# A two-layer encoder on one core: the overflow loop moved into the experts' block, and the last turn's activations moved ahead of a weight split

## The chip, the cores and the metric

The kernel runs on one core of a Trainium2 chip. The metric is the device time of one execution in microseconds. Before the change three runs gave 2638.07, 2639.89 and 2648.47 us, median 2639.89 us.

## What is computed

Layer 0 is differential attention beside a Hyena operator, layer 1 a bidirectional mLSTM. Each layer ends with the same mixture of experts, and only that part is touched:

```python
def hier_moe(x, wg, bg, we, be, w1, w3, w2):      # 1024 tokens of 1024, 4 groups x 8 experts, 2 per token
    ...
    def expert_block(args):
        xe, e = args                              # one block: 128 tokens of one expert
        hid = jax.nn.silu(xe @ w1[e]) * (xe @ w3[e])
        return hid @ w2[e]
    yb = lax.map(expert_block, (xb, blk_e)).reshape(cap, d)
    out = jax.ops.segment_sum(yb * buf_gate[:, None], buf_tok, num_segments=t)
    return out
x = x + hier_moe(rms_norm(x, ffn_norm[layer]), ...)
```

Every expert gets one block of 128 slots. An expert with more than 128 tokens needs another block; such further blocks are the overflow.

## The kernel before

The program is a row of phases. A phase is a block with one hand-written instruction stream for each engine, ordered by semaphores. A phase ends with the block's own join of all engines and then `end_phase()` (lines 108 to 111), a barrier of all engines in which the phase's semaphores are cleared. The phase `experts` (line 1886) is followed by the phase `overflow` (line 2226), once in each layer. After layer 0's overflow comes `ml_values` (line 2391), which begins by reading back the sum that the experts have added to in DRAM; after layer 1's the program ends.

**The experts' phase** takes 32 turns, one for each expert. Per turn GpSimd gathers 128 token rows of `xn_scratch` (`fetch`), TensorE transposes them (`turn_x`), and the weights come in three chunks of 2 MB through a ring of three slots, loaded by SyncE (L1948). Precision is kept by splitting: ScalarE makes the high part of each half chunk (`split`, L2119), VectorE the rest (L2172), and TensorE takes three products, L2038 (high by high), L2040 (rest of x by high) and L2046 (high by rest of w). `silu`, `multiply` and `turn_hid` (L2064) make the transposed hidden activations in PSUM; ScalarE's `move_hid` (L2141) writes `hidH`, VectorE's `move_hid` (L2172, `hidL`) the rest. The output product of expert e runs one turn late. ScalarE scales the result into `y` (`store_y`, L2130), and GpSimd adds it to the rows in DRAM with a scatter (`give`: an index copy at L1999 after the scatter before has landed, then the scatter at L2003).

**The last turn's tail.** After expert 31's gate products only its output product is left. ScalarE's `tail()` (L2159) does in order: split of the last chunk's first half, `store_y` of expert 30, split of the second half, `move_hid` of expert 31, `store_y` of expert 31. VectorE's `tail()` (L2210) does: first half, `multiply`, second half, `move_hid`. TensorE can start its 24 output matmuls only when `hidL` is there; the second 12 also need the second half.

**The queues.** SyncE, behind its ring loads, loads the first overflow expert's three weight chunks (L1975) and, in layer 0, three chunks for the next phases (L171), each after VectorE has finished with the ring slot that it overwrites. GpSimd gathers the first overflow block's rows at L2021, before the last four scatters. So the first overflow block's data are asked for during the experts' phase. The overflow phase waits in GpSimd for all scatters to have landed (`given`, L2277). Then each engine reads the count n of overflow blocks from `ctrl` into a register (L2244), branches (L2245), and loops n times: 8 transposes (L2309), two copies, 16 matmuls in full fp32 that show as 32 in the trace (L2318), silu and product (L2344, L2357), 4 transposes (L2323), a copy, 8 matmuls that show as 16 (L2331), two scalings (L2346, L2361) and one scatter (L2293). While it runs, SyncE loads the next expert's weights and GpSimd gathers the next rows, needed or not. The trace shows that n is 0 in layer 0 and 1 in layer 1: L2309 and its followers run once, near 2600 us.

Of the kernel before, what the change touches and what calls it, by code (L numbers as in the profile page):

```python
# [10 lines left out]
ALU = mybir.AluOpType  # L11
# [3 lines left out]
P = 128  # L15
D = 1024
# [60 lines left out]
def build(nc, I, out):  # L77
    ctx = ExitStack()
    with ctx:
# [1806 lines left out]
        def experts(layer, slots, slot_gate, ctrl, total, xg, y, yidx, oidx, w_over):  # L1886

            (idx_ok, x_lo, x_hi, xh_ok, xl_ok, w_high, w_rest, w_used, silu_ok, hid_ok, h_turned, hh_ok, hl_ok,
             y_moved, met, yidx_ok) = take(16)
            got, gave = gather_in, 16 * NE * layer  # L1890
            got_base = list(gathered)
            s0 = S_MOE1 if layer else S_MOE0
            with ExitStack() as st:
# [10 lines left out]
                LAST = NE - 1  # L1904

# [38 lines left out]
                with nc.Block() as block:  # L1944
# [35 lines left out]

                    @block.gpsimd
                    def _(pool_e):
# [43 lines left out]
                        for e in range(NE - 4, NE):  # L2026
                            give(e % 2, e)

# [78 lines left out]

                    def quarter(bank):
                        return psum[:, bank, :].rearrange("p (k t) -> p k t", k=4)

                    @block.scalar
                    def _(act):
# [53 lines left out]
                        run(act, one, tail)  # L2166

                    @block.vector
                    def _(dve):
# [46 lines left out]
                        run(dve, one, tail)  # L2216
                for b in range(2):
                    gathered[b] += 16 * (NE // 2)
# [3 lines left out]
                end_phase()  # L2222

        @phase
        def overflow(layer, slots, slot_gate, ctrl, total, xgs, idx, w):
            (idx_ok, x_turned, xt_lo, xt_hi, h_ok, silu_ok, hid_ok, h_turned, h_moved, y_ok, ye_lo, ye_hi,
             met) = take(13)
            put = over_given[layer]
            w_in = over_w[layer]  # L2230
            got = over_in[layer]
            with ExitStack() as st:
                nm = str(layer)
                xg = xgs[:, 0, :]
                xgT = sb(st, "oxgT" + nm, [P, KD, P])
                act_h = sb(st, "oact_h" + nm, [P, DE])
                hid = sb(st, "ohid" + nm, [P, DE])
                hidT = sb(st, "ohidT" + nm, [P, 4, P])
                y = sb(st, "oy" + nm, [P, D])

                def run(eng, one, last=None):
                    n = eng.value_load(ctrl[0:1, 0:1], min_val=0, max_val=OVER)  # L2244
                    with eng.If(n > 0):  # L2245
                        with eng.Fori(0, n) as i:
                            one(i)
                            eng.wait_ge(put, 16 * (i + 1))  # L2248
                            eng.sem_inc(met, 1)
                    if last:  # L2250
                        last(n)

                def quarter(bank):
                    return psum[:, bank, :].rearrange("p (k t) -> p k t", k=4)

                with nc.Block() as block:
                    @block.sync
                    def _(sp):
                        def one(i):
                            e = sp.value_load(ctrl[0:1, bass.ds(i + 2, 1)], min_val=0, max_val=NE - 1)  # L2260
                            sp.wait_ge(h_ok, i + 1)
                            for c in range(2):
                                sp.dma_start(w[c], expert_src(layer, e, c)).then_inc(w_in[c], 16)
                            sp.wait_ge(y_ok, i + 1)
                            sp.dma_start(w[2], expert_src(layer, e, 2)).then_inc(w_in[2], 16)

                        def last(n):
                            for c in range(3):
                                sp.wait_ge(w_in[c], 16 * (n + 1))
                                sp.sem_inc(met, 1)  # L2270

                        run(sp, one, last)

                    @block.gpsimd
                    def _(pool_e):

                        pool_e.wait_ge(given, 16 * NE * (layer + 1))  # L2277

                        def one(i):
                            nc.gpsimd.tensor_copy(idx[:, 0:1], slots[:, bass.ds(i + NE, 1)]).then_inc(idx_ok, 1)  # L2280
                            nc.gpsimd.tensor_copy(idx[:, 1:2], slots[:, bass.ds(i + NE + 1, 1)]).then_inc(idx_ok, 1)
                            pool_e.wait_ge(idx_ok, 2 * (i + 1))
                            pool_e.wait_ge(x_turned, i + 1)
                            pool_e.sem_inc(met, 1)
                            pool_e.indirect_dma_start(
                                out=xg, out_offset=None, in_=xn_d[:, :],
                                in_offset=bass.IndirectOffsetOnAxis(ap=idx[:, 1:2], axis=0),
                                bounds_check=T - 1, oob_is_err=False
                            ).then_inc(got, 16)
                            pool_e.wait_ge(ye_lo, i + 1)  # L2290
                            pool_e.wait_ge(ye_hi, i + 1)
                            pool_e.sem_inc(met, 1)  # L2292
                            pool_e.indirect_dma_start(  # L2293
                                out=total[:, :], out_offset=bass.IndirectOffsetOnAxis(ap=idx[:, 0:1], axis=0),
                                in_=y[:], in_offset=None, bounds_check=T - 1, oob_is_err=False,
                                compute_op=ALU.add).then_inc(put, 16)

                        def last(n):
                            pool_e.wait_ge(got, 16 * (n + 1))
                            pool_e.sem_inc(met, 1)  # L2300

                        run(pool_e, one, last)

                    @block.tensor
                    def _(pe):
                        def one(i):
                            pe.wait_ge(got, 16 * (i + 1))
                            for k in range(KD):
                                ins = nc.tensor.transpose(psum[:, k // 4, (k % 4) * P:(k % 4 + 1) * P],  # L2309
                                                          xg[:, k * P:(k + 1) * P], ident[:])  # L2310
                            ins.then_inc(x_turned, 1)
                            pe.wait_ge(xt_lo, i + 1)
                            pe.wait_ge(xt_hi, i + 1)
                            for c in range(2):
                                wc = w[c].rearrange("p (k c) -> p k c", k=8)
                                pe.wait_ge(w_in[c], 16 * (i + 1))
                                for k in range(KD):
                                    ins = nc.tensor.matmul(psum[:, 2 + c, :], xgT[:, k, :], wc[:, k, :],  # L2318
                                                           start=(k == 0), stop=(k == KD - 1))
                            ins.then_inc(h_ok, 1)  # L2320
                            pe.wait_ge(hid_ok, i + 1)
                            for k in range(4):
                                ins = nc.tensor.transpose(psum[:, 4, k * P:(k + 1) * P], hid[:, k * P:(k + 1) * P],  # L2323
                                                          ident[:])
                            ins.then_inc(h_turned, 1)
                            pe.wait_ge(h_moved, i + 1)
                            wc = w[2].rearrange("p (k c) -> p k c", k=4)
                            pe.wait_ge(w_in[2], 16 * (i + 1))
                            for half in range(2):
                                for k in range(4):  # L2330
                                    ins = nc.tensor.matmul(psum[:, 5 + half, :], hidT[:, k, :],  # L2331
                                                           wc[:, k, half * 512:(half + 1) * 512],
                                                           start=(k == 0), stop=(k == 3))
                            ins.then_inc(y_ok, 1)

                        run(pe, one)

                    @block.scalar
                    def _(act):
                        def one(i):  # L2340
# [950 lines left out]
```

## Time and profile before

| what | value |
|---|---|
| median of three runs | 2639.89 us (2638.07 to 2648.47) |
| the profiled execution | 2641.77 us |
| its span in the trace | 2639.9 us |
| TensorE busy | 2399.5 us, 91% |
| VectorE busy | 1823.8 us, 69% |
| ScalarE busy | 1449.9 us, 55% |
| GpSimd busy | 482.4 us, 18% |
| mean DMA rate | 205 GB/s |
| mean granted TensorE clock | 0.95 of full |

Shares of busy time are means over phases with different limits. The chain that ended last starts at 2598.92 us, at the start of layer 1's overflow. Rows are read in microseconds from the start of the span; a granted clock of 1.00 is 2.4 GHz and 0.50 is 1.2 GHz.
### The profile page before, as it was taken

The numbers are of one execution on the slowest core, as the hardware profiler recorded it, in microseconds if no ns is written. First come the engines' busy times: TensorE is split into PE (matmuls) and PEld (weight loads), VectorE is DVE, ScalarE is ACT, GpSimd is POOL, SyncE is SP. The second block draws the span as 40 slices with busy tenths as digits, with TensorE's granted clock in tenths as the row PEclk, the third lists the DMA queues.
The fourth block names the chain that finished last, engine by engine and source line by source line (L and its number), as shares of the span: only waits on it lengthen the run. The fifth ranks groups of instructions, "written<-read, shape, count | busy, mean of one in ns | idle before, by whom it ended". The sixth has DMA issues, their size and how long they took to land. (4 is left out here: it accounts for less than half of the span.)

```text
span 2639.9 us, 32620 instructions
## 1 busy us (share of the span) xinstructions
PE 2399.5 (91%) x11612; PEld 1970.5 (75%) x11612; DVE 1823.8 (69%) x2101; ACT 1449.9 (55%) x1777; POOL 482.4 (18%) x431
## 2 busy tenths in 40 slices
PE   7989989796979999999987998997987999999995
PEld 6768877585867888888865786785776888888882
DVE  6838856578348989888963141478547889888880
ACT  6338742322217878777853231266415788877770
POOL 0001100100002333333310000035201333333220
PEclk9989999897979999999998999998997999999997
DMA  5110011111237999999992221101335999999994
GB/s 177 58 40 1 1 48 36 72 32 37 112 128 304 389 374 394 375 380 387 387 383 93 72 72 56 47 19 46 143 134 213 376 379 382 375 379 388 386 387 155
DMA packets 85912, 542.32 MB, mean 205 GB/s; under 512 B 18996, under 2 KB 22677, under 8 KB 59830
## 3 DMA queue, kind: packets, MB, share of 16 engines
q1 hardware_dynamic: 64358, 502.93, 48.5%
q0 software_dynamic: 19008, 33.61, 5.2%
q10 hardware_dynamic: 2448, 4.46, 0.5%
q8 instruction: 62, 1.02, 0.2%
q14 instruction: 36, 0.29, 0.0%
HBM read 521.52 MB, written 55.05 MB: 218 GB/s over the span
## 5 line engine op out<-in xcount | busy, mean ns | idle before, releaser
L2172 DVE TENSOR_TENSOR wL<-ring,wH 128x2048 fp32r<-128x2048 f32 x384 | 869.4, 2287 | 144.0 <-ACT wH L2119 139.4
L2119 ACT CAST wH<-ring 128x2048 fp32r<-128x2048 f32 x384 | 730.5, 1911 | 213.7 <-DMA ring<-in_moe_w 157.5
L2038 PE MATMUL psum<-wH,xgH 128*128 128x512 f32 x1024 | 407.9, 398 | 12.8 <-DVE xgL L2172 12.6
L2040 PE MATMUL psum<-wH,xgL 128*128 128x512 f32 x1024 | 401.3, 392 | 0.0
L2046 PE MATMUL psum<-wL,xgH 128*128 128x512 f32 x1024 | 275.9, 391 | 0.0
L2038 PEld LDWEIGHTS psum<-wH,xgH 128*128 128x128 f32 x1024 | 193.5, 189 | 56.4 <-DVE xgL L2172 12.5
L2046 PEld LDWEIGHTS psum<-wL,xgH 128*128 128x128 f32 x1024 | 193.4, 189 | 40.8
L2040 PEld LDWEIGHTS psum<-wH,xgL 128*128 128x128 f32 x1024 | 193.8, 189 | 38.2
L2038 PE MATMUL psum<-wH,hidH 128*128 128x512 f32 x512 | 208.1, 406 | 11.0 <-DVE hidL L2172 11.0
L2040 PE MATMUL psum<-wH,hidL 128*128 128x512 f32 x512 | 201.7, 394 | 0.0
L1985 POOL COPY gidx<-slots 128x1 int32 (+1 forms) x60 | 56.1, 935 | 485.8 <-PE psum L2055 485.8
L2046 PE MATMUL psum<-wL,hidH 128*128 128x512 f32 x512 | 138.5, 393 | 0.0
L200 PE MATMUL psum<-xn_high,ring_rest 128*128 128x512 f32 x320 | 127.3, 398 | 0.0
L2038 PEld LDWEIGHTS psum<-wH,hidH 128*128 128x128 f32 x512 | 97.7, 191 | 30.6 <-DVE hidL L2172 11.4
L198 PE MATMUL psum<-w_high_route_rest,y_high_route 128*128 128x512 f32 x256 | 105.8, 413 | 12.3 <-DVE ring_rest L193 11.7
L2046 PEld LDWEIGHTS psum<-wL,hidH 128*128 128x128 f32 x512 | 97.3, 190 | 20.4
L2040 PEld LDWEIGHTS psum<-wH,hidL 128*128 128x128 f32 x512 | 97.8, 191 | 18.6
L200 PE MATMUL psum<-w_high_route_rest,y_rest_route 128*128 128x512 f32 x256 | 102.7, 401 | 0.0
L199 PE MATMUL psum<-ring_rest,y_high_route 128*128 128x512 f32 x256 | 102.6, 401 | 0.0
L199 PE MATMUL psum<-ring_rest,xn_high 128*128 128x512 f32 x256 | 100.9, 394 | 0.0
L2130 ACT ACTIVATE y<-psum,slot_gate 128x1024 f32<-128x1024 f32 x64 | 71.3, 1114 | 52.9 <-PE psum L2046 52.4
L1988 POOL DMA_INDIRECT xg<-xn_scratch,gidx x60 | 90.2, 1503 | 51.3 <-POOL gidx L1985 46.2
(429 smaller groups left out, 4671.2 us busy)
## 6 DMA issues: line engine op xcount, KB each, us to landing
ring<-in_moe_w SPq DMA_DIRECT2D x192, 2048.0 KB
ring<-in_ev_w_in SPq DMA_DIRECT2D x6, 2048.0 KB
xnT<-in_moe_w SPq DMA_DIRECT2D x6, 2048.0 KB, 13.7
ring<-in_od_w_in SPq DMA_DIRECT2D x6, 2048.0 KB
xn_scratch<-xn_route SPq DMA_DIRECT2D x16, 512.0 KB, 2.6
ow<-in_moe_w SPq DMA_DIRECT2D x3, 2048.0 KB, 22.1
v_att<-in_x SPq DMA_DIRECT2D x8, 512.0 KB, 3.8
ring<-in_ev_w_out SPq DMA_DIRECT2D x2, 2048.0 KB
```

The costliest lines, as they stand in the source:

```text
L198: nc.tensor.matmul(dst, lhs[0], rhs[0], start=start, stop=False)
L199: nc.tensor.matmul(dst, lhs[0], rhs[1], start=False, stop=False)
L200: return nc.tensor.matmul(dst, lhs[1], rhs[0], start=False, stop=stop)
L1985: nc.gpsimd.tensor_copy(idx[:, b:b + 1], slots[:, bass.ds(e, 1)]).then_inc(idx_ok, 1)
L1988: pool_e.indirect_dma_start(out=xg[:, b, :], out_offset=None, in_=xn_d[:, :], in_offset=bass.IndirectOffsetOnAxis(ap=idx[:, b:b + 1], axis=0),
L2038: nc.tensor.matmul(psum[:, bank, :], xh[:, k, :], w3[0][:, n, cols], start=(half == 0 and n == 0), stop=False)
L2040: nc.tensor.matmul(psum[:, bank, :], xl[:, k, :], w3[0][:, n, cols], start=False, stop=False)
L2046: ins = nc.tensor.matmul(psum[:, bank, :], xh[:, k, :], w3[1][:, n, cols], start=False, stop=(half == 1 and n == len(ks) - 1))
L2119: nc.scalar.copy(half_of(wH, b, e, c, half), raw(e, c, half)).then_inc(w_high, 1)
L2130: nc.scalar.activation(y[:, b, :], psum[:, 5:7, :].rearrange("p a b -> p (a b)"), ACT.Copy, scale=slot_gate[:, bass.ds(e, 1)]).then_inc(y_ ...
L2172: return nc.vector.tensor_tensor(out, whole, high.bitcast(F32), ALU.subtract)
```

## The change

- The phase `overflow` is gone, with its block and its `end_phase()`. Its loop stands as `further(...)` behind each engine's tail inside the experts' block, so the two phases have one join and one barrier.
- `further` is the old `run`: read n, branch, loop. Its semaphores are 13 others of the same pool. GpSimd waits for the landing of all 32 scatters before it, as before; TensorE now waits for `y_moved` of all experts ahead of the second product.
- `xgT`, `hidT` and `y` of the overflow are allocated in the experts' phase behind its own buffers; `act_h` and `hid` are shared with it.
- In both tails `move_hid(LAST)` now stands ahead of the split of the second half.

```diff
@@ experts @@
+                xgT = sb(st, "oxgT" + nm, [P, KD, P])
+                hidT = sb(st, "ohidT" + nm, [P, 4, P])
+                oy = sb(st, "oy" + nm, [P, D])
+                def further(eng, one, last=None):
+                    n = eng.value_load(ctrl[0:1, 0:1], min_val=0, max_val=OVER)
+                    with eng.If(n > 0):
+                        with eng.Fori(0, n) as i:
+                            one(i)
+                            eng.wait_ge(put, 16 * (i + 1))
+                            eng.sem_inc(further_met, 1)
+                    if last:
+                        last(n)
@@ sync @@
+                        further(sp, block, last)
@@ gpsimd @@
                         for e in range(NE - 4, NE):
                             give(e % 2, e)
+                        pool_e.wait_ge(given, gave + 16 * NE)
+                        pool_e.sem_inc(further_met, 1)
...
+                        further(pool_e, block, last)
@@ tensor @@
                         tail()
+                        def block(i):
+                            pe.wait_ge(further_in, 16 * (i + 1))
...
+                            pe.wait_ge(w_in[2], 16 * (i + 1))
+                            pe.wait_ge(y_moved, NE)
...
+                        further(pe, block)
@@ scalar @@
                         def tail():
                             split(0, LAST + 1, 0, 0)
                             store_y(0, LAST - 1, LAST, 2)
+                            move_hid(LAST)
                             split(0, LAST + 1, 0, 1)
-                            move_hid(LAST)
                             store_y(1, LAST, LAST + 1, 0)
...
+                        further(act, block)
@@ vector @@
                             multiply(LAST)
+                            move_hid(LAST)
                             split(0, LAST + 1, 0, 1)
-                            move_hid(LAST)
...
+                        further(dve, block)
-        @phase
-        def overflow(layer, slots, slot_gate, ctrl, total, xgs, idx, w):
...
-                end_phase()
@@ moe @@
                 experts(layer, slots, slot_gate, ctrl, total, xg, y, yidx, oidx, w)
-                overflow(layer, slots, slot_gate, ctrl, total, xg, oidx, w)
```

## Rows read from the trace of the kernel before

**Rows 1.** which chain ended last: start us, length us, engine and line
```profile
2600.03 1.98 PE psum L2309 x8
...
2602.82 15.39 PE psum L2318 x32
...
2621.05 7.15 PE psum L2331 x16
...
2629.99 1.58 POOL out L2293
```

**Rows 2.** timeline of layer 1's tail: start us, us, engine, line [idle before]
```profile
2573.32 0.60 PE L2064 MATMUL psum<-ident,hid 128*128 128x128 f32 x4
...
2574.53 1.89 ACT L2119 CAST wH<-ring 128x2048 fp32r<-128x2048 f32 x1
...
2576.32 0.59 ACT L2141 CAST hidH<-psum 128x512 fp32r<-128x512 f32 x1
...
2578.66 0.68 DVE L2172 TENSOR_TENSOR hidL<-psum,hidH 128x512 fp32r<-128x512 f32 x1
...
2579.39 0.80 PE L2038 MATMUL psum<-wH,hidH 128*128 128x512 f32 x1 [5.48 <-DVE hidL L2172]
...
2586.76 1.07 PE L2046 MATMUL psum<-wL,hidH 128*128 128x512 f32 x4
2587.87 1.11 ACT L2130 ACTIVATE y<-psum,slot_gate 128x1024 f32<-128x1024 f32 x1 [10.97 <-PE psum L2046]
```

**Rows 3.** sequencer rows, layer 1: engine, ns, start
```profile
L1944 PEldq DRAIN  x1: 5735/5735/5735, 2582.1 to 2582.1; - x1
...
L1944 POOLq DRAIN  x1: 8420/8420/8420, 2589.6 to 2589.6; - x1
...
L2244 PEldq TENSOR_LOAD <-ctrl x1: 310/310/310, 2599.0 to 2599.0; - x1
```

**Rows 4.** granted clock (PEclk), second by second: us, PE busy and others
```profile
1370.00:1371.00 1.00, 0.00 (x0) 0.00 (x0) 0.99 (x2) 0.00 (x0) 0.00 (x0) 0.52 1.00 406
...
1518.00:1519.00 1.00, 0.73 (x3) 0.64 (x4) 1.00 (x2) 1.00 (x2) 0.00 (x0) 1.00 0.00 0
```

**Rows 5.** timeline of PE before the second stretch of the rows above
```profile
1518.27 0.51 PE L198 MATMUL psum<-w_high_o,xn_high 128*128 128x512 f32 x1 [3.27 <-DVE ring_rest L193]
```

**Rows 6.** timeline of GpSimd, end of layer 1: scatters and index copies
```profile
2558.92 2.23 POOL L2003 DMA_INDIRECT out<-y,yidx  x1 [4.91 <-ACT y L2130]
2572.94 0.18 POOL L1999 COPY yidx<-slots 128x1 int32<-128x1 int32 x1 [11.79 <-DMA out<-y,yidx]
2575.50 1.57 POOL L2003 DMA_INDIRECT out<-y,yidx  x1 [2.38 <-ACT y L2130]
2583.87 0.18 POOL L1999 COPY yidx<-slots 128x1 int32<-128x1 int32 x1 [6.79 <-DMA out<-y,yidx]
2589.83 1.57 POOL L2003 DMA_INDIRECT out<-y,yidx  x1 [5.78 <-ACT y L2130]
```

**Rows 7.** the same, end of layer 0
```profile
1375.55 0.18 POOL L1999 COPY yidx<-slots 128x1 int32<-128x1 int32 x1 [6.86 <-DMA x_scratch<-y,yidx]
1381.49 1.57 POOL L2003 DMA_INDIRECT x_scratch<-y,yidx  x1 [5.76 <-ACT y L2130]
```

**Rows 8.** sequencer rows and first DMA of the next phase, layer 0
```profile
L1944 POOLq DRAIN  x1: 10812/10812/10812, 1381.3 to 1381.3; - x1
...
L2244 POOLq TENSOR_LOAD <-ctrl x1: 507/507/507, 1393.0 to 1393.0; - x1
...
L2256 PEldq DRAIN  x1: 63/63/63, 1394.3 to 1394.3; - x1
...
1395.30 0.34 SPq L2429 DMA_DIRECT2D x_ml<-x_scratch  x1
```

**Rows 9.** first TensorE work of each experts phase
```profile
792.55 1.73 PE L2055 MATMUL psum<-ident,xg 128*128 128x128 f32 x7 [3.00 <-PEq L110]
...
2001.45 1.94 PE L2055 MATMUL psum<-ident,xg 128*128 128x128 f32 x8 [3.49 <-PEq L110]
```

More of the change, by code:

```diff
@@ L1889, in experts @@
              y_moved, met, yidx_ok) = take(16)
+            (further_idx, further_x, xt_lo, xt_hi, further_h, further_silu, further_hid, further_turned,
+             further_moved, further_y, ye_lo, ye_hi, further_met) = pool[16:29]
+            put, w_in, further_in = over_given[layer], over_w[layer], over_in[layer]
             got, gave = gather_in, 16 * NE * layer
@@ L1979, in _, with last @@
                                 load_chunk(sp, s0 + 3 * NE + c - 1)
+                        def block(i):
+                            e = sp.value_load(ctrl[0:1, bass.ds(i + 2, 1)], min_val=0, max_val=NE - 1)
+                            sp.wait_ge(further_h, i + 1)
+                            for c in range(2):
+                                sp.dma_start(w_over[c], expert_src(layer, e, c)).then_inc(w_in[c], 16)
+                            sp.wait_ge(further_y, i + 1)
+                            sp.dma_start(w_over[2], expert_src(layer, e, 2)).then_inc(w_in[2], 16)
+                        def last(n):
+                            for c in range(3):
+                                sp.wait_ge(w_in[c], 16 * (n + 1))
+                                sp.sem_inc(further_met, 1)
+                        further(sp, block, last)
                     @block.gpsimd
@@ L2106, in _, with block @@
                         tail()
+                        def block(i):
+                            pe.wait_ge(further_in, 16 * (i + 1))
+                            for k in range(KD):
+                                ins = nc.tensor.transpose(psum[:, k // 4, (k % 4) * P:(k % 4 + 1) * P],
+                                                          xg[:, 0, k * P:(k + 1) * P], ident[:])
+                            ins.then_inc(further_x, 1)
+                            pe.wait_ge(xt_lo, i + 1)
+                            pe.wait_ge(xt_hi, i + 1)
+                            for c in range(2):
+                                wc = w_over[c].rearrange("p (k c) -> p k c", k=8)
+                                pe.wait_ge(w_in[c], 16 * (i + 1))
+                                for k in range(KD):
+                                    ins = nc.tensor.matmul(psum[:, 2 + c, :], xgT[:, k, :], wc[:, k, :],
+                                                           start=(k == 0), stop=(k == KD - 1))
+                            ins.then_inc(further_h, 1)
+                            pe.wait_ge(further_hid, i + 1)
+                            for k in range(4):
+                                ins = nc.tensor.transpose(psum[:, 4, k * P:(k + 1) * P], hid[:, k * P:(k + 1) * P],
+                                                          ident[:])
+                            ins.then_inc(further_turned, 1)
+                            pe.wait_ge(further_moved, i + 1)
+                            wc = w_over[2].rearrange("p (k c) -> p k c", k=4)
+                            pe.wait_ge(w_in[2], 16 * (i + 1))
+                            pe.wait_ge(y_moved, NE)
+                            for half in range(2):
+                                for k in range(4):
+                                    ins = nc.tensor.matmul(psum[:, 5 + half, :], hidT[:, k, :],
+                                                           wc[:, k, half * 512:(half + 1) * 512],
+                                                           start=(k == 0), stop=(k == 3))
+                            ins.then_inc(further_y, 1)
+                        further(pe, block)
                     def quarter(bank):
@@ L2161, in tail, with block @@
                             store_y(0, LAST - 1, LAST, 2)
+                            move_hid(LAST)
                             split(0, LAST + 1, 0, 1)
-                            move_hid(LAST)
                             store_y(1, LAST, LAST + 1, 0)
                         run(act, one, tail)
+                        def block(i):
+                            act.wait_ge(further_x, i + 1)
+                            nc.scalar.copy(xgT[:, 0:4, :], quarter(0)).then_inc(xt_lo, 1)
+                            act.wait_ge(further_h, i + 1)
+                            nc.scalar.activation(act_h[:], psum[:, 2, :], ACT.Silu).then_inc(further_silu, 1)
+                            act.wait_ge(further_y, i + 1)
+                            nc.scalar.activation(oy[:, 0:512], psum[:, 5, :], ACT.Copy,
+                                                 scale=slot_gate[:, bass.ds(i + NE, 1)]).then_inc(ye_lo, 1)
+                        further(act, block)
                     @block.vector
@@ L2221, in experts @@
                     issued[n % RING] = (n if n < S_END else n - RING) // RING + 1
-                end_phase()
-        @phase
-        def overflow(layer, slots, slot_gate, ctrl, total, xgs, idx, w):
[L2227 to L2340, printed above, removed]
-                            act.wait_ge(x_turned, i + 1)
-                            nc.scalar.copy(xgT[:, 0:4, :], quarter(0)).then_inc(xt_lo, 1)
-                            act.wait_ge(h_ok, i + 1)
-                            nc.scalar.activation(act_h[:], psum[:, 2, :], ACT.Silu).then_inc(silu_ok, 1)
-                            act.wait_ge(y_ok, i + 1)
-                            nc.scalar.activation(y[:, 0:512], psum[:, 5, :], ACT.Copy,
-                                                 scale=slot_gate[:, bass.ds(i + NE, 1)]).then_inc(ye_lo, 1)
-                        run(act, one)
-                    @block.vector
-                    def _(dve):
-                        def one(i):
-                            dve.wait_ge(x_turned, i + 1)
-                            nc.vector.tensor_copy(xgT[:, 4:8, :], quarter(1)).then_inc(xt_hi, 1)
-                            dve.wait_ge(silu_ok, i + 1)
-                            nc.vector.tensor_tensor(hid[:], act_h[:], psum[:, 3, :], ALU.mult).then_inc(hid_ok, 1)
-                            dve.wait_ge(h_turned, i + 1)
-                            nc.vector.tensor_copy(hidT[:], quarter(4)).then_inc(h_moved, 1)
-                            dve.wait_ge(y_ok, i + 1)
-                            nc.vector.tensor_scalar(y[:, 512:1024], psum[:, 6, :], slot_gate[:, bass.ds(i + NE, 1)], None,
-                                                    ALU.mult).then_inc(ye_hi, 1)
-                        run(dve, one)
```

31 lines of the change are left out of this document (added).

## The prediction

> **What bounds the kernel now.** I read the chain that ended last first. It begins at the first transposes of layer 1's overflow, at 2600.03 us, and runs down through two products and one scatter [rows 1]. The reader is to see that nothing else ends that late: whatever lets those transposes start earlier moves the end. The chain can't be followed back past that start, so the second view is the timeline in front of it [rows 2], with the sequencers' rows [rows 3]. TensorE's last output matmul of the tail ends at 2587.83 (ScalarE's `store_y` starts 0.04 later, at 2587.87), and TensorE then does nothing for 12.2 us. Who holds it: the scatter is issued at 2589.83 [rows 6], GpSimd's DRAIN at the block's end starts at 2589.6 and lasts 8.42, to 2598.0, and only then does the barrier open; TensorE reads its register at 2599.0 and transposes at 2600.03 [rows 1, 3]. TensorE needs nothing of that scatter. In front of this lies a second hole of 5.48 us, which ends with `hidL` [rows 2]. Layer 0 has the same pattern with another ending: no overflow block runs there, but the next phase reads what the scatter wrote, so the landing is needed. Its rows are 7 and 8.
>
> **Part 1, the tail's new order, in both layers.** Now ScalarE goes from `store_y` of expert 30 into the second split at 2574.53 and reaches `hidH` at 2576.32; the turned activations have been there since 2573.32 + 0.60 = 2573.92 [rows 2]. With the new order `hidH` starts at 2574.53, 1.79 earlier. VectorE starts `hidL` at 2578.66 now, held by its own second split. Afterwards it starts at 2574.53 + 0.59 + 0.04 = 2575.16, which is 3.50 earlier, and TensorE starts 0.73 later (2579.39 - 2578.66), at 2575.89 instead of 2579.39. **3.5 us.**
>
> Moved behind it are the two splits. ScalarE's second split would run from about 2575.05 to 2576.95, VectorE's from 2577.0 to 2579.3 (2.29 to 2.34 with its handover). The second half's rest products come after 12 + 8 matmuls, each 0.23 apart (four in 1.07 us at full clock [rows 2]), so at 2575.89 + 4.6 = 2580.5. The cover is 1.2 us; if it were gone, the cost would be what it is short by. On SyncE's queue layer 0's last ring load waits for that split and would be issued 0.6 us later. I cost this at nothing, because the DMA engines are full then and the load stands in a backlog.
>
> **The clock.** In the last second of the 5.48 us hole the granted clock is down to 0.52, of 1.00 before; the row is layer 0's, whose hole has the same length [rows 4]. A hole of 3.27 us left it at 1.00 [rows 4, 5]. The new hole is 2575.89 - 2573.92 = 1.97 us. So I expect the 24 output matmuls at full clock. Now they take 2587.83 - 2579.39 = 8.44 us; at full clock 24 x 0.23 + 0.15 = 5.65. **2.8 us more.** The tail's matmuls end 6.3 us earlier, at 2581.5 in layer 1.
>
> **Part 2, the joined phases, layer 1.** Between the tail and the transposes remain TensorE's own register load and branch. The old rows say 1.03 us from the start of the load to the first transpose (2599.0 to 2600.03) [rows 1, 3]. That is the upper bound for their visible cost. The lower bound is zero, because the sequencer runs ahead: it stood in the block's DRAIN from 2582.1, while its matmuls ran until 2587.8 [rows 3]. If it can load a register in that time, nothing is left. I take 0.5. By the Trainium skill ("TensorE: Matmul & The Clock Gate", the table at its head) TensorE's queue holds 64 instructions; this case's trace agrees as far as that 5.7 us lead goes, and by it the cost would be near 0.
>
> So the hole of 12.2 becomes 0.5: **11.7 us**. The transposes would start at 2600.03 - 6.3 - 11.7 = 2582.0. The first overflow weights and rows aren't late: they were asked for in the experts' phase, and TensorE would need the third chunk only some 18 us later.
>
> The cold start goes as well. After 12.2 us idle the eight transposes took 1.98 us, and the 32 matmuls of the first product took 15.39, where 16 of the second product took 7.15 [rows 1], so 32 at full clock are about 14.0. **1.0 + 1.4 = 2.4 us.** The last part, from the end of the first product at 2618.2 to the end of the span (21.7 us), stays: the weights for a next block and the scatter collide as they do now.
>
> GpSimd is the queue to look at for the added wait. It waits for expert 31's landing inside the same stream, and behind it stand its index copies, the gather and the final scatter. Expert 31's scatter can't follow `y` all the way: `give` first needs expert 30's scatter landed, at 2583.87 [rows 6], a time that stays. Copy and issue take it to about 2584.9, 4.9 us earlier than 2589.83, not 6.3. It lands 8.4 later (2575.50 to 2583.87 was 8.4), at 2593.3, and GpSimd is ready at about 2596. The overflow's result would need it near 2608. The wait is hidden by 12 us, and TensorE's new wait for `y_moved` by more.
>
> Layer 1 in sum: 6.3 + 11.7 + 2.4 = **20.4 us**. Bounds: 19.8 with the whole register load visible, 20.9 with none.
>
> **Part 3, the joined phases, layer 0.** The scatter moves from 1381.49 to 1375.55 + 1.05 = 1376.6, bounded by the landing before it at 1375.55 [rows 7]: **4.9 us**. Its landing took 1381.3 + 10.8 = 1392.1, less 1381.49, so 10.6 [rows 7, 8]. Under loaded DMA the rows give 8.4 to 14.0 (2558.92 to 2572.94) [rows 6]. I take 10.6, the row nearest in place, with the same loads in flight, so 1387.2. Behind the landing now come join and barrier (0.9, to the register load at 1393.0), load and branch (1.1 to 1.3, to the drains at 1394.1 to 1394.3), then a join and a barrier again (1.0, to 1395.30) [rows 8]. One join and barrier goes, and TensorE's load no longer follows the landing: **1.1 us**. The next phase would start at 1389.3, 6.0 earlier. But its first loads meet the end of the DMA backlog, which was gone by 1395.3; I take 1.0 off for that (0 to 2). Layer 0: **5.0 us**, bounds 2.6 (a landing of 14.0, with no backlog left) and 7.2 (a landing of 8.4, less 1.0 for the backlog).
>
> **The sum** is 20.4 + 5.0 = 25.4 us. Against the profiled execution's own 2641.77 this gives 2616.4; against its span, 2614.5. It lay 1.9 above the median of the runs, and so the median after is 2639.89 - 25.4 = 2614.5. The ratio is 0.990.
>
> **Rivals.**
> - **The clock falls all the same.** For: there is no row of exactly this hole. Against: the 3.27 us hole. Price: 2.8 in layer 1; in layer 0 a tail only 3.5 earlier puts the scatter at 1381.49 - 3.5 = 1378.0 instead of 1376.6, so 1.4; and 2.4 if the overflow starts cold too. Time: 2614.5 + 6.6 = 2621.
> - **Layer 0 gives nothing.** For: the DMA engines are full until about 1390, and the scatter and the next phase's loads share them. Against: even the longest landing of the rows, 14.0, leaves 2.6 us of it [rows 6]. Price 5.0: 2619.5.
> - **The overflow's code isn't there in time.** The wait at the barrier now covers whatever an engine needs to reach the overflow's instructions, and this cover goes. For: nothing in the trace separates it. Against: the code follows in the same stream. Price, taken from the 3.0 to 3.5 us holes at the start of the experts' phases [rows 9] as the farthest bound: 3.0, 2617.5.
> - **Slower: the passes of the experts' loop in layer 1.** Its code lies behind the edit, so it falls on other addresses, and a taken branch at each of TensorE's 13 passes might wait for code. Such a wait decides from 25.4 / 13 = 2.0 us a pass; at 3.3 us a pass the kernel would be at 2657. Against: the two layers' loops already lie at different addresses, and from first transpose to last scatter they take 1381.49 - 792.55 = 588.9 and 2589.83 - 2001.45 = 588.4 [rows 6, 7, 9]. The Trainium skill ("Runtime: NRT & Kernel Launch", section on instruction fetch mechanics) says that a taken branch whose target is outside the fetched window stalls for a fetch. By that rule this rival and the one above could happen; no row here shows such a stall inside the loops.
> - **The join does nothing,** because engines still meet before the overflow. The diff leaves no such wait for TensorE; 11.7 + 1.1 would be missing: 2627.
>
> **How the numbers follow.** Forecast 0.75, clock 0.07, layer 0 nothing 0.08, code 0.04, join nothing 0.02, loops slower 0.03; 0.01 for none of these. The forecast's own range is 2612 (both parts at their good bounds) to 2618. The range goes down to 2610 for the spread of the runs, whose lowest was 1.8 below the median, and up to 2622 to take in the clock, the code and layer 0's rival. A measurement of this kernel tells about 0.5% from no change, 13.2 us, so faster means below 2626.7. Faster 0.94, same 0.03, slower 0.03.
>
> **What would show it right or wrong.** In the tails: `hidL` (L2172's form with 512 columns) right behind `hidH`, a TensorE hole of 2.0 us, 24 matmuls in 5.6 us, a granted clock of 1.00 throughout. In layer 1: transposes of the overflow within 1.1 us of the tail's end, their eight in 1 us, the first product in 14.0, GpSimd's gather well ahead of the final scatter. In layer 0: the last scatter within 1.1 us after the landing before it, and the next phase's first load 2.1 us behind its own landing. The forecast is wrong if TensorE's register load waits for the array and more, if the last scatter of layer 0 lands later than 14 us after its issue, or if the stretch from `ml_values` to the last experts' phase changes its length.

## The result and the profile after

The changed kernel took 2626.75 us (median of 11 runs, 2622.67 to 2636.53), the kernel before, run beside it, 2642.59 (11 runs, 2638.07 to 2648.47). The ratio is 0.9945, 95% interval 0.9935 to 0.9956: about 14.5 us faster. The forecast was 25.4 us (ratio 0.990), with a range for the median of 2610 to 2622. So the direction was right and the time lay outside the range: some 11 us of the gain are missing. The profiled execution took 2623.78 us with a span of 2622.0 us, 17.9 below the span of before.

The timeline of the changed kernel at layer 1's tail answers to [rows 2]:

```profile
2571.73 0.60 PE L2128 MATMUL psum<-ident,hid 128*128 128x128 f32 x4
...
2572.94 0.58 ACT L2238 CAST hidH<-psum 128x512 fp32r<-128x512 f32 x1
2573.40 1.91 ACT L2216 CAST wH<-ring 128x2048 fp32r<-128x2048 f32 x1
2573.55 0.69 DVE L2280 TENSOR_TENSOR hidL<-psum,hidH 128x512 fp32r<-128x512 f32 x1 [4.31 <-ACT hidH L2238]
...
2574.29 0.50 PE L2102 MATMUL psum<-wH,hidH 128*128 128x512 f32 x1 [1.97 <-DVE hidL L2280]
...
2578.96 1.07 PE L2110 MATMUL psum<-wL,hidH 128*128 128x512 f32 x4
2579.87 1.03 PE L2175 MATMUL psum<-ident,xg 128*128 128x128 f32 x8
2580.07 1.11 ACT L2227 ACTIVATE y<-psum,slot_gate 128x1024 f32<-128x1024 f32 x1 [4.75 <-PE psum L2110]
```

`hidL` now follows `hidH` directly, TensorE's hole is the 1.97 us that were worked out, and the overflow's transposes (L2175) start with no hole at all behind the tail. They take 1.03 us instead of 1.98. The chain that ended last answers to [rows 1]; the first product takes 13.99 us instead of 15.39:

```profile
2581.74 13.99 PE psum L2184 x32
...
2598.56 7.15 PE psum L2198 x16
...
2607.48 1.58 POOL out L2082
```

From the end of the first product to the end of the span before took 21.7 us. Here it is 2622.0 - 2595.7 = 26.3. The sequencers' rows of this end say why. L1922 is the instruction right behind each engine's wait for the final scatter's landing, L1964 the block's end (answering to [rows 3], [rows 8]); first the rows of layer 1's end, the last row is layer 0's:

```profile
L1922 POOLq EVENT_SEMAPHORE  x1: 17/17/17, 2615.3 to 2615.3; - x1
...
L1964 POOLq DRAIN  x1: 5362/5362/5362, 2615.7 to 2615.7; - x1
...
L1964 PEldq DRAIN  x1: 8/8/8, 2615.8 to 2615.8; - x1
...
L1964 POOLq DRAIN  x1: 5199/5199/5199, 1382.2 to 1382.2; - x1
```

Everything that GpSimd issued had landed at 2615.3, the other engines' DRAINs take 7 to 17 ns, and still GpSimd's takes 5.36 us. The whole kernel waits for it. Layer 0 shows 5.20 us, at 1382.2. In the kernel before, the DRAIN of the short overflow block took 223 ns in layer 1:

```profile
L2256 POOLq DRAIN  x1: 223/223/223, 2638.8 to 2638.8; - x1
```

So the end has a DRAIN that is 5.1 us longer, and a final landing that was 0.6 us shorter in this trace.

The experts' block's DRAIN of before (8.42 and 10.8 us, rows 3 and 8) lay beside the last scatter's landing and ended behind it. By the semaphore updates in the trace that scatter landed at 2595.41 in layer 1 (5.6 us after its issue) and at 1389.46 in layer 0 (8.0 us after), and the DRAINs ended 2.62 us later in both layers. Layer 1's windows show it too: the DMA engines have nothing left (last but one number, their busy share) while the DRAIN lasts until 2598.0.

```profile
2594.00:2595.00 1.00, 0.00 (x0) 0.00 (x0) 0.00 (x0) 0.00 (x0) 0.00 (x0) 0.50 0.49 90
...
2596.00:2597.00 1.00, 0.00 (x0) 0.00 (x0) 0.00 (x0) 0.00 (x0) 0.00 (x0) 0.50 0.00 0
```

To keep chance out, the kernels below are compared by two edited stretches of their traces: E0, from the end of layer 0's last turned activations (L2064 before) to `ml_values`' first transposes, and E1, from the same point of layer 1 to the end of the span. Between them lies M, from `ml_values`' first transposes to layer 1's first experts' transposes, which the change doesn't touch.

| kernel | runs | mean us | E0 | M | E1 | DRAIN at the joined block's end, layers 0 and 1 |
|---|---|---|---|---|---|---|
| before, three traces | 52 | 2641.4 | 39.1, 37.2, 37.6 | 596.7, 597.8, 601.3 | 66.0, 65.4, 66.1 | none |
| changed, two traces | 17 | 2627.3 | 35.1, 35.2 | 599.9, 603.4 | 49.6, 50.3 | 5199, 5362 ns |
| drain behind the last scatter (e1) | 6 | 2619.8 | 33.4 | 605.4 | 44.6 | 47, 223 ns |
| tail order only (e2) | 5 | 2631.4 | 34.1 | 600.2 | 62.5 | none |
| join only (e3) | 5 | 2629.1 | 38.8 | 599.1 | 55.3 | 5199, 5362 ns |
| drain before the last three (e5) | 6 | 2618.9 | 33.8 | 604.3 | 45.0 | 302, 468 ns |
| index copies doubled (e6) | 1 | 2618.3 | 35.3 | 599.1 | 49.7 | 5199, 5362 ns |
| layer 1 only (e9) | 6 | 2624.8 | 37.3 | 597.5 | 49.6 | -, 5362 ns |
| layer 0 only (e10) | 12 | 2642.6 | 35.1 | 602.6 | 66.0 | 5199 ns, - |
| layer 1 only, drained (e11) | 6 | 2621.2 | 38.1 | 598.9 | 46.3 | -, 468 ns |

The standard error of a mean is 0.6 us for before, 1.2 for the changed kernel, 1.4 for e10, 0.6 for e11 and 1.6 to 2.4 for the others; e6 is a single run.

### The profile page after: what moved, and what is told of

Same layout as the page of the kernel before. It is cut to its first block and busy times, and to the rows that moved or that the text cites. A ratio compares the mean times of both kernels' runs of the same rounds, so it can differ in the third digit from the quotient of the medians.

```text
span 2622.0 us, 32575 instructions
## 1 busy us (share of the span) xinstructions
PE 2392.4 (91%) x11612; PEld 1966.8 (75%) x11612; DVE 1826.0 (70%) x2101; ACT 1452.5 (55%) x1777; POOL 482.4 (18%) x431
## 5 line engine op out<-in xcount | busy, mean ns | idle before, releaser
L2102 PE MATMUL psum<-wH,xgH 128*128 128x512 f32 x1024 | 407.6, 398 | 14.4 <-DVE xgL L2280 14.4
L2034 POOL COPY yidx<-slots 128x1 int32 (+1 forms) x64 | 97.1, 1517 | 56.9 <-DMA out<-y,yidx 33.6
```

What stands on the lines that cost most here:

```text
L2034: nc.gpsimd.tensor_copy(yidx[:, b:b + 1], slots[:, bass.ds(e, 1)]).then_inc(yidx_ok, 1)
L2102: nc.tensor.matmul(psum[:, bank, :], xh[:, k, :], w3[0][:, n, cols], start=(half == 0 and n == 0), stop=False)
```

## The experiments

**A drain in the cover of the last landing.**

```diff
                         for e in range(NE - 4, NE):
                             give(e % 2, e)
+                        pool_e.drain()
                         pool_e.wait_ge(given, gave + 16 * NE)
```

> The changed kernel with one more instruction: GpSimd drains right behind its last scatter's issue, ahead of its wait for the landings. In the changed kernel GpSimd's DRAIN at the joined block's end takes 5.20 us in layer 0 and 5.36 in layer 1, although everything it issued has landed. Theory A: the DRAIN is paid once per indirect DMA (or index copy) since the last DRAIN, about 82 ns each (63 of each in layer 0: 34 + 63 x 82 = 5200; 65 in layer 1: 5364). Then the new DRAIN takes it over while the last scatter is landing (8 us, some 5 of them free), the block's DRAIN falls to 0.03 in layer 0 and 0.2 in layer 1, and the kernel gains 5.2 + 5.1 = 10.3 us against the changed kernel: near 2616. Rival B: the 5.3 us are a price of this block's end, or of something that is only started there; then the block's DRAIN stays near 5.3 in both layers and the time near 2626, or worse by the added DRAIN.

Measured: 2620.92 us (median of 6), ratio to before 0.9918 (0.9900 to 0.9937), some 5 us above the 2616 expected. The added drain and the block's own, in both layers (ns as least, median, most):

```profile
L2065 POOLq DRAIN  x2: 8234/9507/10780, 1375.5 to 2588.2; - x2
```

```profile
L1964 POOLq DRAIN  x2: 47/135/223, 1387.6 to 2620.9; - x2
```

The block's DRAIN falls from 5.2 and 5.4 us to 0.05 and 0.22, and E1 by 5.1 to 5.7. So the time isn't a price of the block's end: it is owed, and whichever drain comes first pays it. The added drain takes 8.2 us in layer 1 and 10.8 in layer 0, the same values as the experts' block's DRAIN before. What sets them is the landing: by the semaphore updates this trace's last scatter lands 5.4 us after its issue in layer 1 and 7.9 in layer 0, and both DRAINs end 2.62 us behind it. In all 13 DRAINs of the traces that stand directly behind a layer's last scatter, with 63 indirect DMAs owed, this distance is 2.62 or 2.63 us. That is half of the 5.20 us that the same 63 cost when nothing is in flight. So only about half of what is owed fits into the cover, and this is why layer 0's first load of the next phase comes 12.8 us after the scatter's issue, 2.6 earlier than in the changed kernel, and not 5.2 as expected.

**The new tail order alone.**

```diff
 # kernel before, ScalarE                    # VectorE
                             store_y(0, LAST - 1, LAST, 2)
+                            move_hid(LAST)
                             split(0, LAST + 1, 0, 1)
-                            move_hid(LAST)
```

> The kernel before with only the new order of the last turn; overflow keeps its phase. By the prediction's part 1: hidL 3.5 us earlier, hole 2.0 instead of 5.5, the last scatter 4.9 us earlier in each layer (bounded by the landing before it). Nothing of the 12.2 us hole's cause goes, so it grows by what TensorE gains on the scatter, and the overflow starts cold. Theory A (the DRAIN's bookkeeping lies beside the landing here): 4.9 per layer, up to 2 more in layer 0 where the landing was slow: 9.8 to 12 us faster than before, about 2631. Rival: the reorder is worth its full 6.3 in each layer (12.6), if the landing before doesn't bind, or under 5 in sum, if layer 0's DMA backlog takes its gain back.

Measured: 2632.21 us (median of 5), ratio 0.9960 (0.9947 to 0.9973). E0 is 3.9 us below the mean of before (38.0), E1 3.3, 7.2 in sum, less than the 9.8 expected. The start of the overflow moves by the scatter's gain, and the 12.2 us hole stays. In layer 1 the clock took something back: this trace's tail ran partly at 1.2 GHz behind the 1.97 us hole, and so did both products (16.89 and 8.71 us, against 15.39 and 7.15 [rows 1], 3.1 more in sum):

```profile
2594.10 1.98 PE psum L2309 x8
...
2596.89 16.89 PE psum L2318 x32
...
2616.62 8.71 PE psum L2331 x16
```

**The join alone** (the changed kernel with `move_hid(LAST)` back behind the second split).

> The changed kernel with the old order of the last turn. Layer 1: the 12.2 us hole goes to 0, the transposes start at full clock (tail cold at first, at full clock for its last third): 12.2 + 2.4 gained, and if theory A holds 5.2 lost at the end: 9.4. If rival B holds and the 5.3 came with the reorder, 14.6. Layer 0: one barrier saved (1.1), against a DRAIN of 5.2 behind the landing instead of beside it: by theory A 2 to 4 us slower than before in this layer; sum 5 to 7 us faster than before, near 2636. With the gains of the order-only kernel the sum should come to what the whole change measured.

Measured: 2628.16 us (median of 5), ratio 0.9960 (0.9947 to 0.9973). E1 falls by 10.5 (65.8 to 55.3; 9.4 expected), E0 rises by 0.9 to 38.8 where a loss of 2 to 4 was expected, and the time is 8 us below the 2636 expected. From the last scatter's issue to the next phase's first load it takes 15.35 us, 1.5 more than the 13.8 to 13.9 of before: one barrier less, and 5.2 us of DRAIN behind the landing instead of 2.62. DRAINs again 5199 and 5362 ns, with the old tail order: they came with the join. The two halves add up, by the stretches: 7.2 + 9.7 = 16.9 against 18.7 for the whole change; the 1.8 between them is less than the 3.1 that the order-only trace lost to the clock in its two products.

**The changed kernel again.**

> The changed kernel once more, unchanged, as the measure beside the other three, and for a second trace of the stretches that the change doesn't touch. The first trace of it was 17.9 us shorter than the one of before; by the edited stretches alone 20.3. If the missing 2.4 are chance, the experts' loop of layer 1 (575.7 us from first transpose to the last turned activations in the first trace, 572.5 before) comes back to other values here, both ways; if code placement costs them, it is again near 575.7 and the kernel before never is.

Measured: 2627.69 us (median of 6), ratio 0.9942 (0.9925 to 0.9960). E0 35.2, E1 50.3, the DRAINs equal to the nanosecond. Layer 1's experts' loop took 575.5 us, as in the first trace (575.7), which is what the expectation called a sign of code placement. But the join-only kernel, whose loop lies behind the same code, took 571.5, and over all runs the eight traces with the join in layer 1 have 571.2 to 575.7 (mean 573.8), the five without it 571.7 to 574.1 (mean 573.3): no clear price of code placement shows. M took 603.4, 2 us above every trace of before.

**The drain moved ahead, three scatters before the end.**

```diff
                         for e in range(NE - 4, NE):
                             give(e % 2, e)
+                            if e == NE - 4:
+                                pool_e.drain()
```

> The changed kernel with GpSimd's own drain placed behind expert 28's scatter, where the engine idles some 9 us for that scatter's landing, instead of behind the last scatter. Theory A (82 ns for each indirect DMA, or each index copy, since the last drain): 3 are left in layer 0 and 5 in layer 1, so the block's DRAIN takes 34 + 3 x 82 = 280 ns in layer 0 and 34 + 5 x 82 = 444 in layer 1. In layer 0 the drain behind the last scatter took 10.8 us and held GpSimd 2.5 us beyond the landing that the changed kernel shows (8.1 us after the issue); that goes, so the stretch from the last turned activations to the next phase's first transposes falls from 33.4 to about 31.2 us, while layer 1's end keeps its gain (21.4 against 26.3 to 26.8 of the changed kernel). Time about 2 us below the 2620.9 of the drain in the cover, beside the spread. Rival B2: what counts is only how long ago the last DRAIN was, or that any was there at all; then the block's DRAIN is 47 and 223 ns again, or another value with no step of 82.

Measured: 2619.14 us (median of 6), ratio 0.9916 (0.9894 to 0.9938). The block's DRAIN with three indirect DMAs since the last one in layer 0, and five in layer 1:

```profile
L1964 POOLq DRAIN  x2: 302/385/468, 1382.0 to 2615.8; - x2
```

Expected were 280 and 444: the step of 83 ns per DMA holds, with a constant some 20 ns larger. With 2, 3, 5, 63 and 65 DMAs the rows say 223, 302, 468, 5199 and 5362 ns, which is 57 to 60 + 81.6 n. The three are three scatters, the two a gather and a scatter, so both kinds cost the same. All of them move 128 rows; whether the price goes by DMA or by row, no run separates. The added drain took 14.1 and 14.2 us and ended 2.50 us behind the landing of expert 28's scatter, with 60 DMAs owed. E0, however, came to 33.8, not 31.2, although the next phase started 2.4 us earlier behind its scatter than with the drain in the cover. Its first load was issued at 1383.16 and used at 1389.74, 6.6 us later:

```profile
1383.16 0.34 SPq L2408 DMA_DIRECT2D x_ml<-x_scratch  x1
...
1389.74 1.06 ACT L2480 ACTIVATE sq_ml<-x_ml 128x1024 f32<-128x1024 f32 x1 [5.52 <-DMA x_ml<-x_scratch]
```

In the kernel before this took 3.9 us (1395.30 to 1399.19; 3.2 in its two other traces), in the changed kernel 3.3, with the drain in the cover 4.2. In e5 the DMA engines are full from 1380 to 1390 (busy share 1.03 to 1.06 as the profile counts it). So an earlier start of `ml_values` does run into the DMA backlog.

**Index copies doubled.**

```diff
+                            nc.gpsimd.tensor_copy(spare[:, b:b + 1], slots[:, bass.ds(e, 1)]).then_inc(yidx_ok, 1)
                             nc.gpsimd.tensor_copy(yidx[:, b:b + 1], slots[:, bass.ds(e, 1)]).then_inc(yidx_ok, 1)
-                            pool_e.wait_ge(yidx_ok, e + 1)
+                            pool_e.wait_ge(yidx_ok, 2 * (e + 1))
```

> The changed kernel with a second index copy, into a spare tile, ahead of each of the 32 scatters of a layer. Indirect DMAs and index copies are equal in number in the changed kernel (63 in layer 0, 65 in layer 1), so its DRAIN can't tell which of them costs 82 ns. If the DMAs do: 5.20 and 5.36 us as before. If the copies, or all GpSimd instructions alike, do: 34 + 95 x 82 = 7.8 us and more in layer 0 for the copies alone, about 6.5 if both kinds share the price.

Measured, 32 more copies in each layer:

```profile
L1965 POOLq DRAIN  x2: 5199/5280/5362, 1379.5 to 2610.3; - x2
```

Not a nanosecond more, in one run (2618.32 us). The indirect DMAs carry the 82 ns, the copies nothing.

**Two more traces of the kernel before.**

> The kernel before, unchanged, for a second trace of its untouched stretch. From the next phase's first transposes in layer 0 to the first transposes of layer 1's experts its first trace took 596.7 us; five traces of kernels with changed ends took 599.1 to 605.4. If that is chance, this trace lies among them; if the earlier start of that stretch costs something in it (a hidden cost of the change), it stays near 597.

> The same as the second trace, once more: with three traces of before against five of the others, chance in the stretch between the two experts' phases would show as overlap (some of before's above 599), a hidden cost of the change as a gap of some 3 to 5 us. The two edited stretches should come out as in the first trace, 39.1 and 66.0 us, within 1 us.

Measured: one run each, 2632.23 and 2644.53 us. M is 597.8 and 601.3. E1 65.4 and 66.1 as expected, E0 37.2 and 37.6, 1.5 to 1.9 below the first trace, so that trace had flattered layer 0's part. M overlaps with the other kernels (599.1 to 605.4) without lying among them.

**The change in one layer only.** A flag `JOINED = layer == 1` (or `== 0`) guards `further`, its buffers and the tail order, and the other layer keeps the old overflow phase; in e11 the early drain is added as well.

> The whole change (join and tail order) in layer 1 alone; layer 0 keeps the form of before. By the edited stretches layer 1 is worth 65.8 - 49.9 = 15.9 us and layer 0 38.0 - 35.2 = 2.8, 18.7 in sum, while the runs say 14.3 (mean of 17 against mean of 33). Theory C: an earlier start of layer 0's next phase is given back in the stretch behind it, and the rest is chance; then this kernel gains as much as the whole change, 14 to 16, near 2626. Theory D: nothing is given back; then it gains 2.8 less than the whole change: 11.5 to 13 by the runs, near 2629. With a standard error of 1.5 to 2 us on each mean only a clear case will tell.

> The whole change in layer 0 alone; layer 1 keeps its form of before. The edited stretch of layer 0 should be near 35.2 us again (38.0 before), layer 1's near 65.8. Theory C (given back behind it): the time is that of before within 1 us, 2641. Theory D: 2.8 faster, 2638.5. A third possibility, that the change in layer 0 costs the missing 4 us in the stretches behind it: slower than before by 1 to 2, 2643, with the stretch between the phases near 603 us against 596.7 to 601.3 in the traces of before.

> The change in layer 1 alone with GpSimd's own drain behind expert 28's scatter, in layer 1. The block's DRAIN at the end of layer 1 falls from 5362 to 468 ns, as it did with the drain in both layers; layer 1's stretch 44.9 us, 20.9 gained, near 2620.5. Against the kernel with both layers changed and drained (2618.9 mean of six) it lacks layer 0's 4.2 us by the stretches: near 2623 if these count in full (theory D), near 2619 to 2620 if they are given back (theory C).

Measured: layer 1 only 2626.15 us (median of 6, ratio 0.9938, 0.9918 to 0.9958), as good as the whole change; layer 0 only 2642.40 (median of 12), ratio 1.0004 (0.9988 to 1.0020), no gain that can be measured: the interval reaches from 3 us faster to 5 slower, so E0's 2.8 is not excluded; layer 1 only with the drain 2621.15 (median of 6, 0.9925, 0.9908 to 0.9942), 2 us from the kernel with both layers drained, which the spread doesn't separate. Its E1 is 46.3, not the 44.9 expected: its tail is one of those that lost 1.6 us to the clock. E0 of the layer-0 kernel did fall to 35.1, but its M is 602.6. Where M loses it: a hole of 3.3 us in TensorE, the one of [rows 5], and the 4.7 us behind it. First the kernel before, then the layer-0 kernel, then e5 (window, its length, busy time of PE, PEld, DVE, ACT, POOL with the number of instructions, then the granted clock, DMA share, GB/s):

```profile
1515.00:1518.30 3.30, 0.03 (x1) 0.03 (x1) 1.31 (x2) 2.39 (x3) 0.00 (x0) 1.00 0.56 199
1518.30:1523.00 4.70, 4.70 (x21) 3.85 (x22) 4.63 (x5) 1.50 (x2) 0.00 (x0) 1.00 0.00 0
```

```profile
1510.10:1513.40 3.30, 0.06 (x1) 0.00 (x0) 1.25 (x2) 2.33 (x3) 0.00 (x0) 1.00 0.56 203
1513.40:1518.10 4.70, 4.67 (x14) 3.76 (x15) 4.67 (x4) 1.56 (x2) 0.00 (x0) 0.64 0.00 0
```

```profile
1505.60:1508.90 3.30, 0.07 (x1) 0.00 (x0) 1.24 (x2) 2.31 (x3) 0.00 (x0) 0.87 0.54 194
1508.90:1513.60 4.70, 4.66 (x11) 3.69 (x12) 4.67 (x4) 1.57 (x2) 0.00 (x0) 0.50 0.00 0
```

The same work gets 21, 14 and 11 matmuls done in 4.7 us. The stretch from that hole to the next long one (103.8 us in the first trace of before) is 105.0 in the layer-0 kernel and 107.8 in e5. Of the five traces whose layer 0 has its old form, three show no matmul at the low clock there; of the seven with the earlier scatter none is free of them. But the join-only trace, whose layer 0 ends no earlier, has six of them too. Over all of M the means are 598.4 us (5 traces) and 602.1 (7; the join-only trace 599.1), and E0 + M together 636.3 and 636.7: in these traces M loses what E0 gains. That part of M's loss is clock is seen in the windows. Whether the clock follows from the earlier start or fell so by chance in these traces stays open; no run separated it.

## Why the prediction was wrong

**Right, to a few tenths.** The tail: `hidL` at once behind `hidH`, a hole of 1.97 us (1.97 worked out), 24 matmuls in 5.7 us (5.65) where the clock stayed full. The second half's split was never late. The join in layer 1: transposes right behind the tail, at the lower bound of the register load's cost. Its row shows the load running while the matmuls still do, 2.2 us before the first transpose:

```profile
L1917 PEldq TENSOR_LOAD <-ctrl x1: 318/318/318, 2577.7 to 2577.7; - x1
```

(The Trainium skill, "TensorE: Matmul & The Clock Gate", gives TensorE's queue 64 instructions; this row agrees that the sequencer can do register work ahead of them.) The warm start was worth 0.95 + 1.4 us (2.4 forecast). Expert 31's scatter was bound by the landing before it, issued 1.4 to 1.5 us behind it (1.05 forecast), and GpSimd was ready for the final scatter 13 us early; that scatter of expert 31 landed 5.5 us after its issue, where 8.4 was forecast.

**The step that failed: "the last part, from the end of the first product at 2618.2 to the end of the span (21.7 us), stays".** I had looked at GpSimd's queue only for what is issued on it. The block's end is an instruction too. The DRAINs of 8.42 us in rows 3 and 10.8 in rows 8 I took whole for the landing, and overlooked that they also worked off what 63 indirect DMAs owe, 5.2 us if nothing is in flight: about half of it in the landing's cover, 2.62 us behind the landing. Joining the blocks moved that DRAIN from beside the last scatter's landing to behind the final landing, with 65 DMAs owed, and all of its 5.36 us stands on the path, where 0.22 stood before. The term was put at nothing without naming what hides it, although rows 3 have the 8.42 us, and the 223 ns DRAIN of the short overflow block in the same trace would have shown the difference. On GpSimd a DRAIN is more than the wait for outstanding work that the section on the profile called it. The Trainium skill ("VectorE: DVE Perf Modes", section "The DRAIN you can't avoid") says of the short DRAINs around a kernel that they take about 12 ns on all five engines. In the changed kernel's trace a barrier's DRAIN takes 7 to 19 ns on the other four engines and 34 to 41 on GpSimd, and GpSimd's at the joined block's end takes up to 5.4 us.

Size of the error in layer 1: E1 fell by 15.8 (65.8 to 50.0), not 20.4. With the drain in the cover it fell by 21.2, so the rest of the sum was right within 1 us.

**Layer 0.** The same term: the "landing of 10.6" was a DRAIN's end, a landing of 8.0 with 2.62 of the DRAIN behind it; now 5.20 stand there, 2.6 more. From the last scatter's issue to the next phase's first load the kernel before needs 13.8 us, the changed one 15.3 (1372.93 to 1388.27), where 12.7 was forecast; with the drain in the cover 12.8, with the early one 10.4. E0 fell by 2.8, not 5.0. A second term shows only with the early drain: the backlog that I priced at 1.0 took 3 us when the start came early enough to meet it. The rival "layer 0 gives nothing", at 0.08, came near in its result: as a whole, layer 0's half brought nothing that could be measured (ratio 1.0004). Its reason, DMA engines shared by scatter and loads, is not what the traces of the changed kernel show; there it is the DRAIN, and M.

**The clock.** (The "seconds" of rows 4 and of the prediction are microseconds.) "I expect the 24 output matmuls at full clock" held in 8 of the 15 tails with the 1.97 us hole; in the other 7 it fell after the first one to five matmuls and stayed low for seven or eight, which cost 1.6 us each. The rival "the clock falls all the same" thus came true in part of the tails. The window of the changed kernel's layer 0 tail:

```profile
1363.60:1371.00 7.40, 7.34 (x24) 5.55 (x24) 2.29 (x1) 1.02 (x2) 1.13 (x1) 0.77 0.99 352
```

One row of a 3.27 us hole at 1.00 wasn't enough for a rule: that same hole, in other traces, is the one shown above at 0.64 and 0.50 behind it.

**The account.** Forecast 25.4, measured 14.2 by the means. Of the missing 11.2, 4.6 lie in E1, 2.2 in E0 and 3.7 in M by the means of traces; 0.7 is inside the errors. The 3.7 is no term of the prediction and its cause is open.

**The other rivals.** Code that isn't there in time, and a join that does nothing: neither shows, as the transposes start with no hole. Of slower loops the means above show no clear sign. The range was too narrow because all its cases kept the block's end as it was, but for the join that does nothing.

**A version faster than both.** The changed kernel with one GpSimd drain placed where that engine idles, behind expert 28's scatter: 2619.14 us, ratio 0.9916 to before. Behind the last scatter it is 2620.92. Against the changed kernel's 17 runs (mean 2627.3) the 12 runs of these two (mean 2619.3) are 8 us faster (standard error 1.9).

## What to carry to other kernels

A barrier is more than its wait: before taking one out, read each engine's DRAIN at it, ask how much of it is landing and how much is owed besides, and see what covers that after the edit. Where GpSimd issues many indirect DMAs, place a drain of its own in an idle stretch before the last one. And a gain at one phase boundary is only a gain if the stretches behind keep their length; changing one site alone and timing it is the test, with enough runs for a gain of that size: twelve were too few for 3 us here.

## What the runs showed that I had not expected

- GpSimd's DRAIN takes about 59 + 81.6 n ns, n being the indirect DMAs that it has issued since its last DRAIN, also when they have all landed (2: 223, 3: 302, 5: 468, 63: 5199, 65: 5362 ns, the same within 1 ns in every trace). 32 more copies on GpSimd change nothing.
- A DRAIN directly behind a scatter ends a fixed time behind that scatter's landing: 2.62 us with 63 indirect DMAs owed (13 DRAINs, 8.2 to 8.4 us long in layer 1 and 10.8 to 10.9 in layer 0), 2.50 with 60 owed (3 DRAINs behind expert 28's scatter, 14.1 to 14.4 us long, while the weights stream). Both are 42 ns per DMA, about half of the 81.6; why half, no run shows.
- The granted clock can fall behind a TensorE hole of 1.97 us: 7 of 15.
